# A decoder layer's ada columns, output projection and first norm: work moved between TensorE, VectorE and GpSimd

## The chip, the cores and the metric

The kernel runs on one core of a Trainium2 chip. Its time is in device microseconds (us). Five engines work beside each other, each through its own list of instructions in order, and wait for each other by semaphores: TensorE (PE, matmuls into PSUM), VectorE (DVE), ScalarE (ACT), GpSimd (Pool) and SyncE (SP), which here only starts DMAs.

## The reference

One decoder layer on x of 512 tokens x 1024, in f32:

```python
mods = silu(c) @ w_ada + b_ada                  # 6 x 1024: sh1, sc1, g1, sh2, sc2, g2
u = x * (1.0 + sc1) + sh1
z = u @ w_in                                    # q, k, v, r, low rank, 3 attention groups, 2 gates
y_gla, y_att = gla(...), dilated_attention(...)
merged = sigmoid(ga) * (y_gla @ w_proj_gla) + sigmoid(gd) * (y_att @ w_proj_attn)
x = layer_norm(alpha * x + g1 * (merged @ w_out), ln1_g, ln1_b)
u = x * (1.0 + sc2) + sh2
y = hier_moe(u, ...)                            # 1 of 4 groups, 2 of its 8 experts per token
x = layer_norm(alpha * x + g2 * y, ln2_g, ln2_b)
```

## The kernel before

**Products.** Each large f32 matmul is done as three in `float32r`: a value is split into a rounded part (`_hi`, a copy on ACT) and a remainder (`_lo`, a subtraction on DVE). Weights come from DRAM by SP in slabs of 128x1024, four to an item of 512 columns, into eight slots. ACT's `slab_hi(j)` and DVE's `slab_lo(j)` split one slab; a slot is reused when the last product that reads it is finished. Products go to PSUM banks 0 and 1 in turn, so product i waits until product i-2 is evacuated.

**Order.** `steps` is one list, written out by hand, that PE, ACT and DVE each walk in the same order, doing their own part of each step: `("z", i)` is a product and its evacuation, `("split", j)` the split of slab j. `zs_next` puts the splits of the next item between the products of this one.

**Start (until 51 us).** The scale and shift of u are the first four blocks of 512 columns of `silu(c) @ w_ada`, in the order `FIRST = (2, 3, 0, 1)`; each comes in two DMAs of 1 MB. For each block DVE multiplies the eight 128x512 slices by a number per partition and adds them (L1364, L1366), and PE sums the result over partitions with four matmuls against a column of ones (L732), so the result stands as columns. DVE adds the bias: `mcol` (L1374, L1377). In the meantime PE has transposed x, ACT copied it out (`xT`, L1022), and split slabs 0 to 3. With `mcol` ACT makes `uT_hi` (L1031), DVE the value of u in place (L1384) and its remainder `uT_lo` (L1391), both behind `uT_hi`. Then DVE splits slabs 0 to 3, and PE runs `lra` and the products of q, k, v and so on.

**Merge and output (611 to 776 us).** Eight `pg` products (y_gla by `w_proj_gla`) are multiplied by their gates on DVE. Between them lie the three parts of `combine`, in which DVE joins the attention groups (`yatt`). PE transposes `yatt` (four steps), and eight `pa` products of half the depth follow: DVE multiplies by the gate (`sgd`, L1306), adds to `mT` (L1308), ACT makes `mT_hi` and DVE `mT_lo` (L1277). The splits of the slabs of `wo` (w_out) lie among the `pa` steps. Eight `wo` products follow, two halves for each 128 tokens. At the first DVE makes the rows of the second modulation, ln1_b * (1+sc2) + sh2 and ln1_g * (1+sc2) (L1318 to L1320). After each pair of halves it has the row statistics (`row_stats`), normalises in place (L1351) and scales twice (L1354, L1355): `u2` for the experts, `x1` for the residual. Pool stores both; PE transposes `u2` and makes the router's logits, which the routing waits for.

**Experts (from 797 us).** A loop over chunks of tokens by expert, the weights split on ACT and DVE as above.

Pool (L568 to L637) starts DMAs: the rows for the modulations, the loads of `x1`, `mods`, `ln_g`, `ln_b` after the last `pg`, and `wr_sb` after the last `pa`.

Of the kernel before, what the change touches and what calls it, by code (L numbers as in the profile page):

```python
# [95 lines left out]
def build(nc, x, c_col, rel_bias, w_ada, b_ada, b_first, w_lra, w_dense, w_gla_gate, b_gla, gla_norm,  # L96
# [254 lines left out]
    between = {2: 0, 3: 1, 5: 2}  # L351
    for ct in range(KD):
        zs_next(("pg", ct, pgn[ct // 4]))
        if ct in between:
            steps.append(("combine", between[ct]))
    for t in range(4):
        z(("yattT", t, None))
    for ct in range(KD):
        if ct < 4:
            split(won[0], ct)  # L360
        elif ct % 2 == 0:
            split(won[1], ct // 2 - 2)
# [66 lines left out]
    fin_in = [sem(f"fin_in{t}") for t in range(NT)]  # L429
# [274 lines left out]
    def _(pe):  # L704
# [17 lines left out]
        for k in range(KD):  # L722
# [4 lines left out]
            last.then_inc(xT_ps, 1)  # L727
        for j in range(4):
# [498 lines left out]
    def _(dve):  # L1227
# [51 lines left out]
        def evac(i):  # L1279
# [31 lines left out]
            else:  # L1311
                t, half = q // 2, q % 2
                hs = slice(512 * half, 512 * half + 512)
                if q == 0:
                    dve.wait_ge(x1_in, 16)
                    dve.wait_ge(mods_in, 48)
                    dve.wait_ge(ln_in, 48)
                    link(dve.tensor_tensor(lnt[0][:, :], ln_b[:, :], mods[:, 2, :], ALU.mult))  # L1318
                    dve.tensor_tensor(mods[:, 1, :], lnt[0][:, :], mods[:, 1, :], ALU.add)
                    dve.tensor_tensor(mods[:, 2, :], ln_g[:, :], mods[:, 2, :], ALU.mult).then_inc(ln_used, 1)  # L1320
# [36 lines left out]
        for j in range(4):
            a = first_acc[j]
            for k in range(KD):
                if k % (KD // 2) == 0:  # L1360
# [11 lines left out]
        dve.wait_ge(small_in, 80)
        dve.wait_ge(col_ps, 2)
        link(dve.scalar_tensor_tensor(out=mcol[:, 0, :], in0=bank(6)[:, 0:KD], scalar=1.0, in1=bcol[:, 0, :],  # L1374
                                      op0=ALU.add, op1=ALU.add))
        dve.wait_ge(col_ps, 4)
        dve.tensor_tensor(mcol[:, 1, :], bank(7)[:, KD:2 * KD], bcol[:, 1, :], ALU.add).then_inc(mcol_rdy, 1)  # L1377
# [4 lines left out]
        def u_value(k):
            dve.wait_ge(u_hi, k + 1)
            dve.tensor_scalar(xT[:, k, :], xT[:, k, :], mcol[:, 0, k:k + 1], mcol[:, 1, k:k + 1], ALU.mult, ALU.add).then_inc(u_val, 1)  # L1384

        u_value(0)
        for k in range(KD):
            if k < KD - 1:
                u_value(k + 1)
            dve.wait_ge(u_val, k + 1)  # L1390
            dve.tensor_tensor(uT_lo[:, k, :], xT[:, k, :], uT_hi[:, k, :].bitcast(f32), ALU.subtract).then_inc(u_lo, 1)  # L1391
# [381 lines left out]
```

## Time and profile before

| | us |
|---|---|
| median of three runs | 1418.17 (1415.79 to 1421.04) |
| profiled execution | 1420.77 |
| its span, first to last instruction | 1418.7 |
| PE busy in the span | 1302.0 (92%) |
| DVE busy | 1023.0 (72%) |
| ACT busy | 691.9 (49%) |
| Pool busy | 364.5 (26%) |

The page of a profile gives busy times, the span in 40 slices, the chain of work that ended last, and groups of instructions. The timeline gives single instructions: start, duration, engine, line, output <- inputs, and in brackets the idle time before it and what ended it. PEld is PE's weight load, SPq the queue of SP. An f32 matmul stands as two records, one in float32r and a transpose as one.

### The profile page before, as it was taken

What the parts mean: (1) busy time and instruction counts of PE and PEld (TensorE: products, weight loads), DVE (VectorE), ACT (ScalarE), POOL (GpSimd) and SP (SyncE); (2) the same over time, 40 slices, a digit from 0 to 9 for tenths busy, and PEclk for the clock granted to TensorE, in tenths of its full rate; (3) what the DMA queues carried; (4) which work ended last, traced back from release to release, by engine and by line L of the source; (5) the groups of instructions that cost most, each with busy time, mean ns of one, the idle gap of its engine ahead of it and who ended that gap; (6) DMA issues with size and microseconds to landing.
All of it is one profiled execution on the core that took longest, in us unless ns stands there. A gap on an engine that the chain in (4) does not pass through costs nothing.

```text
span 1418.7 us, 18051 instructions
## 1 busy us (share of the span) xinstructions
PE 1302.0 (92%) x6280; PEld 1057.1 (75%) x6280; DVE 1023.0 (72%) x1103; ACT 691.9 (49%) x846; POOL 364.5 (26%) x210
## 2 busy tenths in 40 slices
PE   4899899999999999999897499999999999999990
PEld 2577676667898898888676478888888888888870
DVE  6777657744443333337697779999999999999975
ACT  2422344434333433461312267777777777777740
POOL 0100000000000000000001315655665656655532
PEclk8899999999999999999997599999999999999995
DMA  9985311103203223252516589999999999999923
GB/s 348 368 293 201 119 61 58 45 16 119 75 16 119 66 82 109 73 181 92 204 67 270 212 313 362 371 374 371 366 363 368 365 382 367 376 368 370 363 70 121
DMA packets 72866, 314.43 MB, mean 222 GB/s; under 512 B 14898, under 2 KB 15058, under 8 KB 47984
## 3 DMA queue, kind: packets, MB, share of 16 engines
q1 hardware_dynamic: 57488, 283.36, 53.6%
q0 software_dynamic: 14752, 28.29, 6.5%
q10 hardware_dynamic: 576, 2.10, 0.4%
q8 instruction: 33, 0.54, 0.1%
q14 instruction: 17, 0.14, 0.0%
HBM read 313.58 MB, written 28.95 MB: 241 GB/s over the span
## 4 chain that ended last, share of the span: by engine, by line
PE 81%; DVE 10%; ACT 3%; SPq 2%; issue 2%; DMA 2%; DVEq 0%; POOLq 0%; ACTq 0%
PE ps L945 12%; PE ps L947 12%; PE ps L946 12%; PE ps L739 11%; PE ps L741 10%; PE ps L740 10%; PE ps L866 2%; PE ps L935 2%; PE ps L908 1%; DVE d_lo L1245 1%; PE ps L844 1%; PE ps L841 1%; PE ps L962 1%; SPq L485 1%; PE ps L878 1%
## 5 line engine op out<-in xcount | busy, mean ns | idle before, releaser
L1634 DVE TENSOR_TENSOR w_lo<-w_raw,w_hi 128x2048 fp32r<-128x2048 f32 x192 | 433.1, 2286 | 24.6 <-ACT w_hi L1156 24.6
L1156 ACT CAST w_hi<-w_raw 128x2048 fp32r<-128x2048 f32 x192 | 357.3, 1917 | 0.0
L945 PE MATMUL ps<-w_hi,xT_hi 128*128 128x512 f32 x512 | 207.4, 405 | 2.4 <-DVE xT_lo L1647 2.4
L673 POOL DMA_INDIRECT y_d<-yb,ui x32 | 167.4, 5231 | 163.2 <-DVE yb L1642 138.7
L947 PE MATMUL ps<-w_hi,xT_lo 128*128 128x512 f32 x512 | 201.6, 394 | 0.0
L946 PE MATMUL ps<-w_lo,xT_hi 128*128 128x512 f32 x512 | 200.5, 392 | 0.0
L1245 DVE TENSOR_TENSOR d_lo<-d_raw,d_hi 128x1024 fp32r<-128x1024 f32 x96 | 115.1, 1222 | 75.8 <-ACT d_hi L1018 74.9
L739 PE MATMUL ps<-uT_hi,d_hi 128*128 128x512 f32 x384 | 155.7, 405 | 0.2 <-DVE d_lo L1245 0.2
L741 PE MATMUL ps<-uT_hi,d_lo 128*128 128x512 f32 x384 | 151.1, 393 | 0.0
L740 PE MATMUL ps<-uT_lo,d_hi 128*128 128x512 f32 x384 | 150.8, 393 | 0.0
L945 PEld LDWEIGHTS ps<-w_hi,xT_hi 128*128 128x128 f32 x512 | 97.1, 190 | 21.3 <-DVE xT_lo L1647 2.8
L947 PEld LDWEIGHTS ps<-w_hi,xT_lo 128*128 128x128 f32 x512 | 96.7, 189 | 21.4
L946 PEld LDWEIGHTS ps<-w_lo,xT_hi 128*128 128x128 f32 x512 | 97.4, 190 | 18.8
L945 PE MATMUL ps<-w_hi,hT_hi 128*128 128x512 f32 x256 | 100.5, 393 | 2.0 <-DVE hT_lo L1672 2.0
L739 PE MATMUL ps<-d_hi,uT_hi 128*128 128x512 f32 x224 | 93.9, 419 | 9.0 <-DVEq L1295 6.4
L1018 ACT CAST d_hi<-d_raw 128x1024 fp32r<-128x1024 f32 x96 | 97.7, 1043 | 6.4 <-DMA d_raw<-in 4.9
L946 PE MATMUL ps<-w_lo,hT_hi 128*128 128x512 f32 x256 | 100.4, 392 | 0.0
L947 PE MATMUL ps<-w_hi,hT_lo 128*128 128x512 f32 x256 | 100.4, 392 | 0.0
L605 POOL DMA_DIRECT2D bias<-brep_d x3 | 2.7, 908 | 352.0 <-DVE sm L1481 188.3
L740 PE MATMUL ps<-d_lo,uT_hi 128*128 128x512 f32 x224 | 89.4, 399 | 0.0
L739 PEld LDWEIGHTS ps<-uT_hi,d_hi 128*128 128x128 f32 x384 | 72.8, 190 | 22.1 <-issue 5.8
L741 PE MATMUL ps<-d_hi,uT_lo 128*128 128x512 f32 x224 | 89.3, 399 | 0.0
(312 smaller groups left out, 2173.5 us busy)
## 6 DMA issues: line engine op xcount, KB each, us to landing
w_raw<-in SPq DMA_DIRECT2D x192, 1024.0 KB, 7.3
d_raw<-in SPq DMA_DIRECT2D x96, 512.0 KB, 3.6
ada_buf<-in SPq DMA_DIRECT2D x8, 2048.0 KB, 8.9
ada_w<-in SPq DMA_DIRECT2D x8, 1024.0 KB, 14.1
att_d<-Og POOLq DMA_DIRECT2D x2, 1056.0 KB, 7.6
O<-att_d POOLq DMA_DIRECT2D x2, 1056.0 KB, 8.2
x_in<-in SPq DMA_DIRECT2D x1, 2048.0 KB, 13.7
brep_d<-bvec_d POOLq DMA_DIRECT2D x2, 1024.0 KB, 19.1
```

The costliest lines, as they stand in the source:

```text
L673: pool.indirect_dma_start(y_d, bass.IndirectOffsetOnAxis(ap=idxs[s], axis=0), yb[s][:, :], None, bounds_check=S - 1, oob_is_err=False, com ...
L739: pe.matmul(dst, a_hi, b_hi, start=first, stop=False)
L740: pe.matmul(dst, a_hi, b_lo, start=False, stop=False)
L741: return pe.matmul(dst, a_lo, b_hi, start=False, stop=final)
L866: last = pe.matmul(dst, lhs, rhs, start=True, stop=True)
L945: pe.matmul(dst, a_hi[:, k, :], hi[:, w], start=(k == 0), stop=False)
L946: pe.matmul(dst, a_hi[:, k, :], lo[:, w], start=False, stop=False)
L947: last = pe.matmul(dst, a_lo[:, k, :], hi[:, w], start=False, stop=(k == a_hi.shape[1] - 1))
L1018: act.copy(d_hi[j % SLOTS][:, :], d_raw[j % SLOTS][:, :]).then_inc(d_hi_rdy, 1)
L1156: act.copy(w_hi[n % NHI][:, :], w_raw[j][:, :]).then_inc(w_hi_rdy, 1)
L1245: dve.tensor_tensor(d_lo[j % SLOTS][:, :], d_raw[j % SLOTS][:, :], d_hi[j % SLOTS][:, :].bitcast(f32), ALU.subtract).then_inc(d_lo_rdy, 1)
L1634: dve.tensor_tensor(w_lo[j][:, :], w_raw[j][:, :], w_hi[n % NHI][:, :].bitcast(f32), ALU.subtract).then_inc(w_lo_rdy, 1)
```

## The change

- **Ada columns.** Of the four first blocks, DVE sums blocks 0 and 2 (`ON_DVE`) as before. Blocks 1 and 3 are multiplied and summed on PE: for each half of a block that has landed and each 128 columns, four matmuls with the weights as stationary operand and a column of silu(c) as moving one. The two halves stand in separate PSUM columns, and DVE adds them with one more operation for each of the two rows of `mcol`.
- **u.** ACT makes `uT_hi` ahead of the copies of slabs 0 to 3 instead of behind them. The values of u go to a tile of their own, `u_f32`, and no longer wait for `uT_hi`; DVE makes the first five, Pool the last three.
- **combine** stands after `pg` products 0, 2 and 4 instead of 2, 3 and 5.
- **Splits of `wo`.** Slab 0 ahead of the transposes of y_att, 1 among them, 2 behind them, 3 at the second `pa`, instead of one at each of the first four `pa`. The others stay.
- **Norm rows.** The three operations L1318 to L1320 are on Pool, behind the landing of their inputs. The load of `wr_sb` stands behind them in Pool's order.
- **Norm.** Instead of one normalising operation and two of two for scaling, `normed` does (v - mean) * g and then * rstd + b, for `u2` and for `x1`: four operations where five were.
- The semaphores of the first DMAs serve for those of the last tiles too.

```diff
-    between = {2: 0, 3: 1, 5: 2}
+    between = {0: 0, 2: 1, 4: 2}
...
+    split(won[0], 0)
     for t in range(4):
         z(("yattT", t, None))
+        if t == 1:
+            split(won[0], 1)
+    split(won[0], 2)
     for ct in range(KD):
-        if ct < 4:
-            split(won[0], ct)
-        elif ct % 2 == 0:
+        if ct == 1:
+            split(won[0], 3)
+        if ct in (4, 6):
             split(won[1], ct // 2 - 2)
...
         pool.wait_ge(mcol_rdy, 1)
+
+        pool.wait_ge(xT_sb, KD)
+        for k in range(U_POOL, KD):
+            pool.tensor_scalar(u_f32[:, k, :], xT[:, k, :], mcol[:, 0, k:k + 1], mcol[:, 1, k:k + 1], ALU.mult, ALU.add).then_inc(u_val_pool, 1)
...
+        pool.wait_ge(mods_in, 48)
+        pool.wait_ge(ln_in, 32)
+        link(pool.tensor_tensor(lnt[1][:, :], ln_b[:, :], mods[:, 2, :], ALU.mult))
+        pool.tensor_tensor(mods[:, 1, :], lnt[1][:, :], mods[:, 1, :], ALU.add)
+        link(pool.tensor_tensor(mods[:, 2, :], ln_g[:, :], mods[:, 2, :], ALU.mult))
+        pool.sem_inc(ln_used, 1)
...
         for j in range(4):
-            pe.wait_ge(first_sum, j + 1)
-            for q in range(4):
-                n = 4 * j + q
-                last = pe.matmul(bank(6 + j // 2)[:, n:n + 1], first_acc[j][:, P * q:P * q + P], ones[:, 0:1], start=True, stop=True)
+            dst = bank(6 + j // 2)
+            if j in ON_DVE:
+                pe.wait_ge(first_sum, ON_DVE.index(j) + 1)
+                for q in range(4):
+                    n = 4 * j + q
+                    last = pe.matmul(dst[:, n:n + 1], first_acc[j][:, P * q:P * q + P], ones[:, 0:1], start=True, stop=True)
+            else:
+                for h in range(2):
+                    pe.wait_ge(half_in[2 * j + h], 16)
+                    for q in range(4):
+                        n = 4 * j + q + 16 * h
+                        for k in range(KD // 2 * h, KD // 2 * h + KD // 2):
+                            last = pe.matmul(dst[:, n:n + 1], ada_w[j][:, k, P * q:P * q + P], csil[:, k:k + 1],
+                                             start=(k % (KD // 2) == 0), stop=(k % (KD // 2) == KD // 2 - 1))
             last.then_inc(col_ps, 1)
...
-        act.wait_ge(first_sum, 1)
-        for j in range(4):
-            slab_hi(j)
         act.wait_ge(mcol_rdy, 1)
         act.wait_ge(xT_sb, KD)
         for k in range(KD):
             act.activation(uT_hi[:, k, :], xT[:, k, :], ACT.Identity, bias=mcol[:, 1, k:k + 1], scale=mcol[:, 0, k:k + 1]).then_inc(u_hi, 1)
+        for j in range(4):
+            slab_hi(j)
...
-                    norm_rows(x1[:, t, :])
-                    scale_rows(u2[:, t, :], x1[:, t, :], mods[:, 2, :], mods[:, 1, :]).then_inc(u2_rdy, 1)
+                    row_stats(x1[:, t, :], lrs)
+                    normed(u2[:, t, :], x1[:, t, :], mods[:, 2, :], mods[:, 1, :]).then_inc(u2_rdy, 1)
...
+        def normed(o, v, g, b):
+
+            link(dve.scalar_tensor_tensor(out=o, in0=v, scalar=bnag[:, 0:1], in1=g, op0=ALU.subtract, op1=ALU.mult))
+            return dve.scalar_tensor_tensor(out=o, in0=o, scalar=lrs, in1=b, op0=ALU.mult, op1=ALU.add)
...
-        for j in range(4):
+        for j in ON_DVE:
...
         def u_value(k):
-            dve.wait_ge(u_hi, k + 1)
-            dve.tensor_scalar(xT[:, k, :], xT[:, k, :], mcol[:, 0, k:k + 1], mcol[:, 1, k:k + 1], ALU.mult, ALU.add).then_inc(u_val, 1)
+            dve.tensor_scalar(u_f32[:, k, :], xT[:, k, :], mcol[:, 0, k:k + 1], mcol[:, 1, k:k + 1], ALU.mult, ALU.add).then_inc(u_val, 1)
```

## Rows read from the trace of the kernel before

**Rows 1.** The page's part 4: the chain that ended last, by engine.
```profile
PE 81%; DVE 10%; ACT 3%; SPq 2%; issue 2%; DMA 2%; DVEq 0%; POOLq 0%; ACTq 0%
```

**Rows 2.** The timeline until 51 us: start, duration, engine, line, operation.
```profile
19.25 0.49 DVE L1364 TENSOR_SCALAR first_acc<-ada_w,sm 128x512 f32<-128x512 f32 x1 [4.36 <-DMA ada_w<-in]
...
31.60 5.47 DVE L1366 SCALAR_TENSOR_TENSOR first_acc<-ada_w,sm,first_acc 128x512 f32<-128x512 f32 x7
...
39.08 1.04 ACT L1018 CAST d_hi<-d_raw 128x1024 fp32r<-128x1024 f32 x1 [0.24 <-DMA d_raw<-in]
39.10 0.17 DVE L1377 TENSOR_TENSOR mcol<-ps,bcol 128x8 f32<-128x8 f32 x1 [1.96 <-PE ps L732]
...
40.03 5.75 ACT L1031 ACTIVATE uT_hi<-xT,mcol 128x512 fp32r<-128x512 f32 x8
...
50.90 0.50 PE L739 MATMUL ps<-uT_hi,d_hi 128*128 128x512 f32 x1 [0.18 <-DVE d_lo L1245]
```

**Rows 3.** The timeline of PE's matmuls, 22 to 44 us.
```profile
23.14 0.95 PE L732 MATMUL ps<-cst,first_acc 128*128 128x1 f32 x8
...
37.13 1.87 PE L732 MATMUL ps<-cst,first_acc 128*128 128x1 f32 x8 [4.04 <-DVE first_acc L1366]
```

**Rows 4.** Stretches: length, busy PE, PEld, DVE, ACT, Pool (x count), clock, DMA, GB/s.
```profile
23.00:25.00 2.00, 1.09 (x11) 1.01 (x9) 1.93 (x3) 0.76 (x2) 0.00 (x0) 1.00 1.05 386
25.00:27.00 2.00, 1.69 (x8) 1.69 (x8) 1.93 (x4) 0.00 (x0) 0.00 (x0) 0.54 1.06 388
...
45.60:46.00 0.40, 0.40 (x4) 0.09 (x1) 0.40 (x2) 0.18 (x1) 0.00 (x0) 0.95 1.03 412
...
100.00:120.00 20.00, 20.00 (x88) 16.21 (x87) 14.95 (x19) 5.56 (x7) 1.45 (x3) 1.00 0.63 218
...
766.00:770.00 4.00, 1.02 (x5) 1.02 (x6) 3.93 (x4) 0.00 (x0) 0.53 (x1) 0.50 1.01 428
...
796.00:802.00 6.00, 0.00 (x0) 0.00 (x0) 6.00 (x5) 0.00 (x0) 4.50 (x3) 0.50 0.11 29
```

**Rows 5.** The timeline of PE, 756 to 776 us.
```profile
763.65 1.98 PE L707 MATMUL ps<-wr_sb,u2T 128*128 128x36 f32 x16 [0.73 <-ACT u2T L1136]
768.98 1.97 PE L886 MATMUL ps<-cst,u 128*128 128x128 f32 x8 [3.36 <-DVE u L1355]
```

**Rows 6.** The chain of work in order of time, 600 to 800 us: start, length, what.
```profile
792.15 3.72 PE ps L926 x16
```

**Rows 7.** The timeline of DVE, 596 to 800 us.
```profile
689.08 1.22 DVE L1245 TENSOR_TENSOR d_lo<-d_raw,d_hi 128x1024 fp32r<-128x1024 f32 x1 [1.64 <-ACT d_hi L1018]
...
716.95 1.22 DVE L1318 TENSOR_TENSOR lnt<-ln_b,mods 128x1024 f32<-128x1024 f32 x1
...
720.60 0.69 DVE L1323 TENSOR_TENSOR lnt<-ps,mods 128x512 f32<-128x512 f32 x1
...
727.42 0.81 DVE L1351 TENSOR_SCALAR x<-x,sm 128x1024 f32<-128x1024 f32 x1
```

**Rows 8.** The timeline of PE, 677 to 716 us: the first matmul of the fifth `pa`.
```profile
695.32 0.50 PE L739 MATMUL ps<-yattT_hi,d_hi 128*128 128x512 f32 x1 [1.29 <-DVEq L1307]
```

**Rows 9.** The timeline of DVE, 1385 to 1420 us.
```profile
1405.00 1.28 DVE L1712 SCALAR_TENSOR_TENSOR ya<-ya,sm,ln2gb 128x1024 f32<-128x1024 f32 x1
1406.20 3.36 DVE L1710 SCALAR_TENSOR_TENSOR ya<-ya,sm,ln2gb 128x1024 f32<-128x1024 f32 x1
```

**Rows 10.** The timeline of Pool, 1370 to 1420 us.
```profile
1405.20 3.28 POOL L700 TENSOR_TENSOR ya<-ya,ln2gb 128x1024 f32<-128x1024 f32 x1 [18.00 <-ACT ya L1220]
1408.56 3.20 POOL L701 TENSOR_TENSOR ya<-ya,ln2gb 128x1024 f32<-128x1024 f32 x1
```

**Rows 11.** The timeline of Pool, 596 to 800 us.
```profile
775.32 1.96 POOL L640 MEMSET xg<- 128x1024 f32 x2 [3.17 <-PE ps L707]
```

**Rows 12.** The instructions that touch `ln_b`: its load and that DMA's time to landing.
```profile
L627 POOL DMA_DIRECT2D ln_b<-in x1: 528/528/528, 681.6 to 681.6; - x1
...
DMA to landing us min/median/max: 15.5/15.5/15.5
```

More of the change, by code:

```diff
@@ L128, in build @@
     x_in = at("x_in", 112, [P, NT, D])
+    u_f32 = at("u_f32", 112, [P, KD, S])
+    U_POOL = 5
     ada_w = [at(f"ada_w{b}", kb, [P, KD, 512]) for b, kb in enumerate((64, 80, 160, 176))]
@@ L399, in build @@
     csil_act = sem("csil_act")
-    first_in = [sem(f"first_ada_in{n}") for n in range(8)]
+    half_in = [sem(f"first_ada_half_or_last_tile_in{n}") for n in range(8)]
     xT_ps, xT_sb, col_ps, mcol_rdy = sem("xT_ps"), sem("xT_sb"), sem("mod_cols_ps"), sem("mod_cols")
     first_sum = sem("first_ada_sum")
-    FIRST = (2, 3, 0, 1)
+    FIRST, ON_DVE = (2, 3, 0, 1), (0, 2)
+    csil_rdy = sem("csil_rdy")
     out_rdy, out_act, out_dve, sig_rdy = sem("out_rdy"), sem("out_freed_act"), sem("out_freed_dve"), sem("sig_rdy")
@@ L428, in build @@
     y_st = [sem("y_store0"), sem("y_store1")]
-    fin_in = [sem(f"fin_in{t}") for t in range(NT)]
     fin_rdy, ln2_in, last_rdy = sem("fin_rdy"), sem("ln2_in"), sem("last_rdy")
@@ L484, in _ @@
                 ks = slice(KD // 2 * h, KD // 2 * h + KD // 2)
-                sp.dma_start(ada_w[j][:, ks, :], cols(w_ada, 512 * b)[:, ks, :]).then_inc(first_in[2 * j + h], 16)
+                sp.dma_start(ada_w[j][:, ks, :], cols(w_ada, 512 * b)[:, ks, :]).then_inc(half_in[2 * j + h], 16)
             if j == 0:
@@ L1241, in _ @@
         link(dve.tensor_tensor(csil, csil, ccol, ALU.mult))
+        dve.sem_inc(csil_rdy, 1)
         def slab_lo(j):
@@ L1315, in evac @@
                     dve.wait_ge(x1_in, 16)
[L1316 to L1320, printed above, removed]
                     dve.wait_ge(ln_used, 1)
@@ L1371, in _ @@
                     ins.then_inc(first_sum, 1)
[L1372 to L1377, printed above, removed]
         dve.wait_ge(lra_hi_rdy, 1)
         dve.tensor_tensor(lra_lo[:, :, :], lra_w[:, :, :], lra_hi[:, :, :].bitcast(f32), ALU.subtract).then_inc(lra_lo_rdy, 1)
+        dve.wait_ge(small_in, 80)
+        for m, add in ((0, 1.0), (1, 0.0)):
+            dve.wait_ge(col_ps, 2 * m + 2)
+            c = bank(6 + m)
+            link(dve.scalar_tensor_tensor(out=mcol[:, m, :], in0=c[:, KD * m:KD * m + KD], scalar=add, in1=bcol[:, m, :],
+                                          op0=ALU.add, op1=ALU.add))
+            ins = dve.tensor_tensor(mcol[:, m, KD // 2:KD], mcol[:, m, KD // 2:KD],
+                                    c[:, 16 + KD * m + KD // 2:16 + KD * m + KD], ALU.add)
+            if m == 0:
+                link(ins)
+            else:
+                ins.then_inc(mcol_rdy, 1)
         dve.wait_ge(mcol_rdy, 1)
+        dve.wait_ge(xT_sb, KD)
         def u_value(k):
-            dve.wait_ge(u_hi, k + 1)
-            dve.tensor_scalar(xT[:, k, :], xT[:, k, :], mcol[:, 0, k:k + 1], mcol[:, 1, k:k + 1], ALU.mult, ALU.add).then_inc(u_val, 1)
+            dve.tensor_scalar(u_f32[:, k, :], xT[:, k, :], mcol[:, 0, k:k + 1], mcol[:, 1, k:k + 1], ALU.mult, ALU.add).then_inc(u_val, 1)
         u_value(0)
         for k in range(KD):
-            if k < KD - 1:
+            if k < U_POOL - 1:
                 u_value(k + 1)
-            dve.wait_ge(u_val, k + 1)
-            dve.tensor_tensor(uT_lo[:, k, :], xT[:, k, :], uT_hi[:, k, :].bitcast(f32), ALU.subtract).then_inc(u_lo, 1)
+            if k < U_POOL:
+                dve.wait_ge(u_val, k + 1)
+            else:
+                dve.wait_ge(u_val_pool, k - U_POOL + 1)
+            dve.wait_ge(u_hi, k + 1)
+            dve.tensor_tensor(uT_lo[:, k, :], u_f32[:, k, :], uT_hi[:, k, :].bitcast(f32), ALU.subtract).then_inc(u_lo, 1)
         for j in range(4):
```

18 lines of the change are left out of this document (7 added, 11 removed).

## The prediction

> **What bounds the kernel now.** I read the page's chain first [rows 1]: TensorE (PE) holds 81% of it and VectorE (DVE) 10%. So a microsecond saved on another engine counts only where PE waits for that engine, and a microsecond added ahead of PE's first dense work counts in full if PE is dense afterwards. It is: in the stretch from 100 to 120 us PE is busy for 20.00 of 20.00 us [rows 4]. The change touches two places where PE does wait, so I then read the timeline of the first 51 us and that of the output projection (677 to 776 us).
>
> In the first place the ada columns come out of four weight blocks. DVE multiplies and adds eight slices for each block, 0.49 us and then 7 in 5.47 us; the fourth block's seven start at 31.60 and `mcol` is finished at 39.10 + 0.17 = 39.27 [rows 2]. At 40.03 ACT starts the eight `uT_hi`, after its last slab copy (39.08 + 1.04) [rows 2], and the first product of q starts at 50.90 [rows 2]: T + 11.6, with T = 39.27 for `mcol`. In the second place DVE and ACT hold PE up: PE stood for 1.29 us ahead of the fifth product of `pa` [rows 8], because of the slab splits between the gates.
>
> **Edit 1: blocks 1 and 3 summed on PE. The price of one call.** A call is an f32 matmul with a 128x128 stationary block of `ada_w` and one moving column of `csil`. The trace has this very shape, L732: four calls are 8 records, and take 0.95 us at 23.14 and 1.87 us at 37.13 [rows 3]. The clock tells them apart: granted 1.00 from 23 to 25 us and falling to 0.50 after (mean 0.54 from 25 to 27) [rows 4], that is 2.4 against 1.2 GHz. So a call costs 0.24 us at 2.4 GHz and 0.47 us at 1.2 GHz, although one column moves: the stationary side is what is paid. Block 1 now needs 2 halves x 4 quarters x 4 slices = 32 calls where it had 4, and block 3 the same: 7.7 or 14.9 us for each block.
>
> Which clock? PE will be busy without a break, but with one-column work. I read what such work did to the clock. Before 25 us it did transposes and eight records of one column, then little, and the clock fell. After a run of sixteen 128x36 matmuls that ended at 763.65 + 1.98 = 765.63 the clock was 0.50 in the next stretch [rows 5, 4]. Sixteen short matmuls without a pause, 3.72 us at 792.15 [rows 6], didn't lift it: 0.50 from 796 to 802 [rows 4]. The 128x512 matmuls of `lra` did: 0.95 in the stretch from 45.6 us on [rows 4]. I therefore take 1.2 GHz from 25.2 us on. This is the choice on which the forecast hangs.
>
> Order on PE: the transposes end at 23.14, block 0 takes 0.95 (24.1); block 1 runs 1.1 us at the high clock (9 of its 64 records) and 55 records x 1.87/8 = 12.9 us at the low one: 38.1. Block 2's sum must be there: its halves land at 24.7 and 27.4, since the first half of block 1 was there at 19.25 [rows 2] and at 386 GB/s [rows 4] a 1.05 MB half takes 2.7 us; DVE ends it near 30.7, unwaited for. Block 2 takes 1.9 (40.0), block 3 64 x 0.234 = 15.0 (its last half landed near 32.8, so it isn't late): 55.0. Two short column operations on DVE instead of one, 0.17 us each as at 39.10 [rows 2], give T = 55.3. **Against 39.27 that is +16.0 us.** DVE has 2 x 5.96 us less to do, but stands idle for it: its sums are not what is late. Bounds: if the clock falls some us later, each us at the high clock saves one; I allow 3, so +13 to +17. If it never falls: 24.1 + 7.7 + 1.0 + 7.7 + 0.3 = 40.8, +1.5.
>
> The Trainium skill speaks against my choice: "TensorE: Matmul & The Clock Gate", section "Why this matters for your kernels", has it that keeping TensorE continuously busy brings the full clock. The row at 792.15 disagrees, with 3.72 us of work and 0.50 behind it; by the rule the sum would be the rival below.
>
> **Edit 2: u by three engines, slab copies behind it.** ACT starts `uT_hi` at T + 0.05 instead of T + 0.76 and takes 0.72 a piece; its first slab copy ends at T + 6.9, in time. DVE does five values (0.46 each, back to back) and eight remainders (0.60) instead of eight and eight, but no longer waits for `uT_hi` at the start. Pool makes three values 128x512. The trace shows none; the nearest rows are its memset of 128x1024, 1.96 us for two [rows 11], so 0.5 us for half of one, and its two-input 128x1024, 2.2 us alone (below), so 1.1 for half. I take the middle, 0.8. Pool's operation and DVE's with two SBUF inputs don't run side by side (next edit), so I add them: the first remainder at T + 1.0, four values and seven remainders more, Pool's three 0.8 each in between: last remainder at T + 9.7, first `d_lo` at T + 10.8. Against T + 11.6 **-0.8 us** (0 to -1.7 for 1.1 and 0.5). DMAs that wait for `mcol` (`gn_b`, `mrow`, the `brep` copies behind Pool's three operations) are needed 100 us later.
>
> "GPSIMD Engine Reference" of the Trainium skill, section 3.1, gives 0.77 us for 512 elements in its best loop; by it the sum would be the same.
>
> **Edit 3: norm rows folded on Pool.** DVE loses three operations at 716.95 until 720.60 [rows 7], 3.65 us. What Pool's cost is shows at the end of the trace. Pool's 128x1024 product was issued at 1405.20 while DVE's operation of 1405.00 ran (1.28 us, until 1406.28), and ended at 1408.48: 2.2 us alone [rows 9, 10]. DVE's next, of 1406.20, took 3.36 us instead of 1.28, so it waited until Pool had finished; Pool's second, of 1408.56, then ended 2.2 us after DVE's end at 1409.56 [rows 9, 10]. So whoever has begun keeps the other out. The inputs land at 681.6 + 15.5 = 697.1 [rows 12]: Pool runs three times 2.2 us from 697 on, in the midst of `pa`, where DVE's `mT`, `mT_lo` and `d_lo` have two SBUF inputs. I followed DVE, ACT and PE in order through this stretch with durations of [rows 7, 8]; the same recurrence, run for the order of before, ends the last remainder of m at 714.3 and the last logits at 775.2, as the trace has them.
>
> **Edit 4: slab splits and combines earlier.** Three of the six splits of `wo` within `pa` go. A step with a split is a chain of 4.3 us: twice 0.69 and 0.15 for the gate (a 128x512 operation takes 0.69 at 720.60), 0.5 for ACT's `mT_hi`, half of a slab copy, 1.04 for that copy and 1.14 to 1.22 for `d_lo`, as at 689.08 [rows 7]. One without is three operations of 0.69 on DVE, 2.05. Two cycles saved give -4.5; the two splits now among the transposes of y_att cost +0.6: -3.9 for the last `mT_lo`, 710.4. The combines stay beside PE's dense `pg` products, whose banks DVE can empty one product late: nothing, and if one came too late, the wait of DVE behind it would be PE's.
>
> With Pool in it: its 6.6 us cost DVE 4.9 (the rest falls beside `sgd`, which reads PSUM, and waits for ACT). The last `mT_lo` is at 715.3, the second product of `wo` ends at 722.0 and DVE's second evacuation at 723.7, where it was: the 3.65 us removed only replace a wait for PE.
>
> **Edit 5: norm in two operations.** For each row tile the 0.81 us operation at 727.42 [rows 7] and four of 1.23 become four of 1.28. Ahead of the fourth u2 that is -0.7 us, and another 0.5 comes from bank waits that PE has less of. The last transposes start at 768.98 [rows 5]; now at 767.5. **Edits 3 to 5: -1.2 us**, to -6.1 if Pool does not hold DVE up, to 0 if it does so more.
>
> **Sum:** +16.0 - 0.8 - 1.2 = +14.0 us. The profiled execution took 1420.77 (span 1418.7, and 2.1 around it): 1434.8. It lies 2.6 above the median of the runs, 1418.17, so for a median I say **1432**. Own range: +13 - 1.7 - 6.1 to +17, 1423 to 1435.
>
> **Rivals.** (a) The clock stays at 2.4 GHz through the one-column work. For it: PE has no pause. Against it: the three rows above. Then +1.5 - 0.8 - 1.2 = -0.5, 1418, between 1412 and 1421: not slower. It decides as soon as PE's records of block 1 keep 0.12 us each beyond 26 us. (b) A call that adds to the same column costs less than one that stands alone. No row has this. At its limit the last half's landing decides, T = 32.8 + 0.9: -5.6 - 0.8 - 1.2 = -7.6, 1410.6, faster. Against it: 128x36 matmuls, which do add up eight deep, cost 1.98/16 = 0.12 us a record [rows 5], no less than L732. (c) The clock falls, but returns or stays for part of the 64 + 64 records: half of the price, +6, about 1424. (d) Edits 3 to 5 give their whole 6.1 us because Pool gets its turns where DVE idles; with the forecast's start that is 1427, in its own range.
>
> **Chances.** The forecast with (d) 0.76, (a) 0.10, (b) 0.05, (c) 0.09. Low end 1420, to hold (c) and part of (a), high end 1436. This kernel's measurement can tell about 0.5% from nothing, 7.1 us: slower than 1425.3 is the forecast less its lowest end, 0.74, and a third of (c), 0.03; faster than 1411.1 is (b), 0.05; the rest is 0.18.
>
> **What would show it.** Right: PE's records of the ada columns at 0.23 us with a granted clock of 0.50, `mcol` near 55 us, the first q product near 66; DVE idle from 31 us. Pool's three products of 2.2 to 3.3 us around 697 to 706 with DVE operations of 2 to 3 us beside them; wo's second evacuation still near its old place, apart from the shift of the start. Wrong: records of 0.12 us with clock 1.00, or far fewer us for 64 records, or DVE operations of 0.7 us beside Pool's.

## The result, and the profile after

The changed kernel takes 1429.53 us (median of 6 runs, 1428.89 to 1430.12), the kernel before 1419.16 us beside it (6 runs, 1415.79 to 1421.04): a ratio of 1.0071, 95% interval 1.006 to 1.0081. It is slower by 10.4 us. The profiled execution of after took 1428.89 (span 1426.7), that of before 1420.77 (span 1418.7): 8.1 apart, less than the medians, because before's was one of its slower runs and after's its fastest.

By engine, the chain of after against [rows 1]: PE's share has grown by four points, DVE's and ACT's have shrunk.

```profile
PE 85%; DVE 9%; ACT 2%; DMA 2%; issue 1%; SPq 0%; DVEq 0%; POOLq 0%; ACTq 0%
```

The two places of the change, first the ada columns. The timeline of PE's matmuls of after, 19 to 51 us (start, duration, line, count), answers to [rows 3]:

```profile
18.70 3.95 PE L743 MATMUL ps<-cst,x_in 128*128 128x128 f32 x22
22.49 0.95 PE L752 MATMUL ps<-cst,first_acc 128*128 128x1 f32 x8
23.30 10.92 PE L759 MATMUL ps<-sm,ada_w 128*128 128x1 f32 x64
34.08 1.85 PE L752 MATMUL ps<-cst,first_acc 128*128 128x1 f32 x8
35.78 13.79 PE L759 MATMUL ps<-sm,ada_w 128*128 128x1 f32 x64
```

L759 is the new work, block 1 and block 3. The stretches of after over the same time (length, busy PE, PEld, DVE, ACT, Pool with counts, granted clock, DMA, GB/s) answer to [rows 4]:

```profile
22.40:25.00 2.60, 2.60 (x27) 2.60 (x25) 0.44 (x1) 0.81 (x2) 0.00 (x0) 1.00 1.05 388
25.00:28.00 3.00, 3.00 (x23) 3.00 (x22) 2.86 (x5) 0.00 (x0) 0.00 (x0) 0.75 1.05 386
28.00:31.00 3.00, 3.00 (x16) 3.00 (x15) 2.45 (x4) 0.00 (x0) 0.00 (x0) 0.50 1.05 386
...
36.00:40.00 4.00, 4.00 (x20) 4.00 (x21) 0.00 (x0) 0.00 (x0) 0.00 (x0) 0.50 1.03 418
45.00:49.00 4.00, 4.00 (x20) 4.00 (x21) 0.00 (x0) 0.00 (x0) 0.00 (x0) 0.50 0.98 360
```

PE is busy for every microsecond of it, and the granted clock falls all the same, from 2.4 to 1.2 GHz between 25 and 28 us, and stays there. The records come at 27 in 2.60 us before the fall and at 16 in 3.00 us behind it. DVE and Pool wait for it. Their timelines of after, 49 to 62 us, against [rows 2]:

```profile
49.68 0.17 DVE L1398 SCALAR_TENSOR_TENSOR mcol<-ps,bcol 128x8 f32<-128x8 f32 x1 [14.77 <-PE ps L759]
49.88 0.16 DVE L1400 TENSOR_TENSOR mcol<-mcol,ps 128x4 f32<-128x4 f32 x1
...
50.99 1.10 DVE L1421 TENSOR_TENSOR uT_lo<-u_f,uT_hi 128x512 fp32r<-128x512 f32 x1
52.02 0.54 DVE L1410 TENSOR_SCALAR u_f<-xT,mcol 128x512 f32<-128x512 f32 x1
52.47 1.09 DVE L1421 TENSOR_TENSOR uT_lo<-u_f,uT_hi 128x512 fp32r<-128x512 f32 x1
...
55.42 3.08 DVE L1421 TENSOR_TENSOR uT_lo<-u_f,uT_hi 128x512 fp32r<-128x512 f32 x5
```
```profile
50.23 4.27 POOL L585 TENSOR_SCALAR u_f<-xT,mcol 128x512 f32<-128x512 f32 x3 [36.46 <-DVE mcol L1400]
```

DVE stood idle for 14.77 us and `mcol` was ready at 49.88 + 0.16 = 50.04 instead of 39.27. The first product of q started at 60.20 instead of 50.90: 9.3 us of the loss are there by 61 us.

The second place. Pool's three new operations, then what DVE (696 to 736 us) and PE (710 to 716 us) did meanwhile, in the timelines of after, against [rows 7, 8]:

```profile
704.39 2.58 POOL L641 TENSOR_TENSOR lnt<-ln_b,mods 128x1024 f32<-128x1024 f32 x1 [13.99 <-DMA ln_b<-in]
707.05 2.73 POOL L642 TENSOR_TENSOR mods<-lnt,mods 128x1024 f32<-128x1024 f32 x1
709.74 2.79 POOL L643 TENSOR_TENSOR mods<-ln_g,mods 128x1024 f32<-128x1024 f32 x1
```
```profile
704.02 0.68 DVE L1305 TENSOR_TENSOR mT_lo<-mT,mT_hi 128x512 fp32r<-128x512 f32 x1
704.62 0.68 DVE L1334 TENSOR_TENSOR sgd<-ps,sgd 128x512 f32<-128x512 f32 x1
705.45 2.06 DVE L1336 TENSOR_TENSOR mT<-mT,sgd 128x512 f32<-128x512 f32 x1
707.44 2.89 DVE L1305 TENSOR_TENSOR mT_lo<-mT,mT_hi 128x512 fp32r<-128x512 f32 x1
710.25 3.35 DVE L1273 TENSOR_TENSOR d_lo<-d_raw,d_hi 128x1024 fp32r<-128x1024 f32 x1
...
727.99 0.69 DVE L1346 TENSOR_TENSOR lnt<-ps,mods 128x512 f32<-128x512 f32 x1
728.72 0.69 DVE L1347 SCALAR_TENSOR_TENSOR x<-x,lnt 128x512 f32<-128x512 f32 x1
733.33 0.69 DVE L1346 TENSOR_TENSOR lnt<-ps,mods 128x512 f32<-128x512 f32 x1 [3.92 <-PE ps L769]
```
```profile
714.32 0.80 PE L767 MATMUL ps<-yattT_hi,d_hi 128*128 128x512 f32 x1 [4.49 <-DVEq L1335]
```

The same `mT_lo` takes 0.68 us when it starts ahead of Pool's first operation and 2.89 beside the second, and PE then waits 4.49 us. DVE has lost the 3.65 us of the row operations of [rows 7], and waits 3.92 us for PE at the second evacuation of `wo`. From the first `pg` evacuation to the first exponential of the routing the trace has 137.39 us before (639.68 to 777.07) and 138.93 after (647.96 to 786.89).

### The profile page after: what moved, and what is told of

It is laid out like the page before. It is cut to its first block, busy times and chain, and to the rows that moved or that the text cites. A ratio compares the mean times of both kernels' runs of the same rounds, so it can differ in the third digit from the quotient of the medians.

```text
span 1426.7 us, 18264 instructions
## 1 busy us (share of the span) xinstructions
PE 1321.9 (93%) x6392; PEld 1079.1 (76%) x6392; DVE 1011.2 (71%) x1079; ACT 692.2 (49%) x846; POOL 370.7 (26%) x216
## 4 chain that ended last, share of the span: by engine, by line
PE 85%; DVE 9%; ACT 2%; DMA 2%; issue 1%; SPq 0%; DVEq 0%; POOLq 0%; ACTq 0%
PE ps L973 12%; PE ps L975 12%; PE ps L974 12%; PE ps L767 12%; PE ps L769 11%; PE ps L768 11%; PE ps L894 2%; PE ps L963 2%; PE ps L759 2%; PE ps L936 1%; PE ps L872 1%; PE ps L869 1%; PE ps L990 1%; DVE d_lo L1273 1%; DMA x_in<-in 1%
## 5 line engine op out<-in xcount | busy, mean ns | idle before, releaser
L690 POOL DMA_INDIRECT y_d<-yb,ui x32 | 161.0, 5033 | 159.4 <-DVE yb L1672 134.9
L1046 ACT CAST d_hi<-d_raw 128x1024 fp32r<-128x1024 f32 x96 | 97.7, 1043 | 16.8 <-DMA d_raw<-in 15.2
## 6 DMA issues: line engine op xcount, KB each, us to landing
x_in<-in SPq DMA_DIRECT2D x1, 2048.0 KB, 13.7
```

The source lines that it names most:

```text
L690: pool.indirect_dma_start(y_d, bass.IndirectOffsetOnAxis(ap=idxs[s], axis=0), yb[s][:, :], None, bounds_check=S - 1, oob_is_err=False, com ...
L1046: act.copy(d_hi[j % SLOTS][:, :], d_raw[j % SLOTS][:, :]).then_inc(d_hi_rdy, 1)
```

## The experiments

Two theories stood. A: the ada sums on PE are the whole loss, 10.7 us as seen at `mcol`, and everything else is a small gain. C: Pool's fold of the norm rows holds DVE up and eats what edits 3 to 5 would give. The rivals were that the late edits or a shifted clock cause the loss, and that Pool's part is harmless.

**Ada sums back on DVE, all else as changed.** The second column operation stays, as an addition of zero. The cuts of the code here and below show the lines that matter; "..." stands where some are left out.

```diff
-    FIRST, ON_DVE = (2, 3, 0, 1), (0, 2)
+    FIRST, ON_DVE = (2, 3, 0, 1), (0, 1, 2, 3)
...
```

> The changed kernel with all four ada blocks summed on VectorE again (the PE sums undone), all else of the change kept. Theory A (the price of the 64 one-column calls on PE is the whole loss): mcol is ready at 39.3 us instead of 50.04, and everything behind it moves by 10.7 us: 1429.5 - 10.7 = 1418.8, equal to the kernel before within 2 us. Rival B (the loss lies mostly in the late edits): 1424 or more.

Measured: 1415.86 us (10 runs), ratio 0.9985 (0.997 to 1.0001), 13.7 below the changed kernel by the medians. `mcol` was ready at 39.68, the first q product started at 50.36, 9.8 earlier than in after. Theory A holds: the loss is gone. The median is 2.9 below the 1418.8 that theory A gave; the part on the prediction says what that difference is made of. Pool and DVE still held each other up, since Pool still folds the rows; the timeline of this kernel, 692 to 700 us:

```profile
694.86 0.69 DVE L1305 TENSOR_TENSOR mT_lo<-mT,mT_hi 128x512 fp32r<-128x512 f32 x1
...
695.91 2.40 POOL L641 TENSOR_TENSOR lnt<-ln_b,mods 128x1024 f32<-128x1024 f32 x1 [14.66 <-DMA ln_b<-in]
...
696.29 2.57 DVE L1336 TENSOR_TENSOR mT<-mT,sgd 128x512 f32<-128x512 f32 x1
```

**Edit 1 alone.** The kernel before, with blocks 1 and 3 summed on PE and nothing else.

> The kernel before with nothing but blocks 1 and 3 summed on PE. Theory A: mcol ready near 50 us, first q product at 50.0 + 11.6 = 61.6 or somewhat sooner, because the slab copies are done by then (uT_hi starts 0.7 earlier after mcol): 60.9; time 1419.2 + 10.0 to 10.7 = 1429.5. Rival B: below 1425.

Measured: 1430.23 us (4 runs), ratio 1.0071 (1.0043 to 1.0099), 11.2 above the kernel before. `mcol` was ready at 52.40 (+13.1) and the first q product started at 63.28 (+12.4), both more than 2 us later than expected. Its block 1 took more than after's, 13.01 us, because the clock fell sooner: the mean granted clock was 0.72 from 24 to 25 us and 0.50 from 25 us on. In the timeline of PE's matmuls, 20 to 66 us:

```profile
23.56 13.01 PE L742 MATMUL ps<-sm,ada_w 128*128 128x1 f32 x64
36.43 1.84 PE L735 MATMUL ps<-cst,first_acc 128*128 128x1 f32 x8
38.14 13.79 PE L742 MATMUL ps<-sm,ada_w 128*128 128x1 f32 x64
```

Edit 1 by itself makes the loss. Block 3 costs 13.79 us in both kernels; when the clock falls differs from one trace to the next, and nothing here shows why.

**Can filling work hold the clock?** After every four calls, one 128x512 matmul into a bank that nobody reads, and one of 16 columns behind each block; that work is extra. It reads a piece of `uT_hi` that ACT copies out of x first, and PE waits for that copy ahead of block 0.

```diff
+        pe.wait_ge(warm_rdy, 1)
...
+                        pe.matmul(bank(0), uT_hi[:, 0, 0:P], uT_hi[:, 0, :], start=True, stop=True)
...
```

> The changed kernel with one extra 128x512 float32r matmul into an unused bank after every four of the one-column calls (8 more for each block), whose result nobody reads. Theory A1 (the calls of block 1 and 3 are slow because the granted clock falls to 1.2 GHz during one-column work): the clock stays at 1.00, a call costs 0.24 us, a block 7.7 + 8 x 0.23 = 9.5 us, mcol is ready at 23.4 + 9.5 + 1.0 + 9.5 + 0.4 = 43.8 us instead of 50.0, time 1429.5 - 6.2 = 1423.3. Rival A2 (the calls cost what they cost, whatever the clock): 16 x 0.4 us more work, mcol at 56, time 1436.

Measured: 1441.73 us (4 runs), ratio 1.0164 (1.0142 to 1.0186), beyond both theories' numbers. The clock was not held. The stretches of this kernel:

```profile
25.00:28.00 3.00, 3.00 (x17) 2.90 (x16) 2.86 (x5) 0.00 (x0) 0.00 (x0) 0.54 1.05 386
28.00:31.00 3.00, 3.00 (x16) 2.90 (x14) 2.59 (x4) 0.00 (x0) 0.00 (x0) 0.50 1.05 386
```

PE had paused 1.24 us just before, for the copy that the edit itself brought in (22.4 to 25 us: 1.17 busy of 2.60), so this doesn't tell whether the filling would hold a clock that is up; it didn't lift one that was down, in 36 us. A group of eight records with its filling came every 2.13 us (29.47, 31.60, 33.73), about 0.4 more than eight records back to back in after (8 x 0.215).

**One block on PE instead of two.** Block 1 on PE, block 3 back on DVE.

```diff
-    FIRST, ON_DVE = (2, 3, 0, 1), (0, 2)
+    FIRST, ON_DVE = (2, 3, 0, 1), (0, 2, 3)
...
```

> The changed kernel with only block 1 on PE, blocks 0, 2 and 3 on VectorE. VectorE's third sum ends at 24.6 + 2 x 5.96 = 36.5, PE has been done with block 1 since 34.2, then four calls for block 2 and four for block 3, 1.9 us each at 1.2 GHz: mcol at 38.4 + 0.4 = 38.8. Theory A: 1429.5 - 11.2 = 1418.3. Rival: the sum of three blocks on VectorE is late by itself and mcol is no sooner than 42: 1421 or more.

Measured: 1417.68 us (10 runs), ratio 0.9992 (0.9978 to 1.0006); `mcol` at 40.56 (38.8 was expected), 0.9 behind the kernel with all four on DVE. The first q product started at 50.21, no later than the 50.36 of that kernel. Its timelines, 20 to 50 us, PE and DVE:

```profile
23.91 12.76 PE L759 MATMUL ps<-sm,ada_w 128*128 128x1 f32 x64
36.53 3.55 PE L752 MATMUL ps<-cst,first_acc 128*128 128x1 f32 x16
```
```profile
31.10 2.33 DVE L1386 SCALAR_TENSOR_TENSOR first_acc<-ada_w,sm,first_acc 128x512 f32<-128x512 f32 x3
34.26 3.11 DVE L1386 SCALAR_TENSOR_TENSOR first_acc<-ada_w,sm,first_acc 128x512 f32<-128x512 f32 x4 [0.84 <-DMA ada_w<-in]
```

The first block's 12.8 us on PE lie beside DVE's sums, which end at 37.37, and cost nothing that the time shows; only the second block, whose weights land last, has nothing beside it. That is where the price is paid.

**The other operand order.** The same sums with `silu(c)` as the one-column stationary operand and the 128x512 slices of `ada_w` moving: 8 calls for a block, a copy of the row by ACT, and 4 calls that turn it back into columns.

```diff
...
-                            last = pe.matmul(dst[:, n:n + 1], ada_w[j][:, k, P * q:P * q + P], csil[:, k:k + 1], ...
...
+                    last = pe.matmul(bank(j // 2)[0:1, :], csil[:, k:k + 1], ada_w[j][:, k, :], ...
...
```

> The changed kernel with the operands of the ada calls swapped: the column of silu(c) is stationary, 128x512 slices of the block move (8 calls of 512 columns for a block instead of 32 of one), ACT copies the row out of PSUM, four calls of one row turn it into columns. Theory A (the price is the stationary loads, doubled because one-column work lets the clock fall): the clock stays at 1.00 through block 1; a record of 512 f32 columns takes 0.43 us at 2.4 GHz (33x384 took 0.64 at 1.2), 16 records 6.8 us; mcol near 23.4 + 6.8 + 0.7 + 0.5 + 0.95 + 6.8 + 0.7 + 0.5 + 0.4 = 40.8 us, time 1429.5 - 9.2 = 1420.3. Rival (PE is throttled by something else, the DMA load or f32 itself): the clock is 0.50, 13.6 us a block, mcol at 54, time 1433.

Measured: 1421.27 us (10 runs), ratio 1.0022 (1.0007 to 1.0037), 8.3 below the changed kernel. Its timeline of PE's matmuls and two of its stretches:

```profile
23.99 7.03 PE L757 MATMUL ps<-ada_w,sm 128*1 128x512 f32 x16
31.69 1.05 PE L762 MATMUL ps<-cst,first_acc 1*128 1x1 f32 x8 [0.67 <-ACT first_acc L1054]
32.66 1.05 PE L752 MATMUL ps<-cst,first_acc 128*128 128x1 f32 x8
33.65 7.03 PE L757 MATMUL ps<-ada_w,sm 128*1 128x512 f32 x16
```
```profile
25.00:28.00 3.00, 3.00 (x9) 0.59 (x7) 2.86 (x5) 0.00 (x0) 0.00 (x0) 1.00 1.05 387
37.00:40.00 3.00, 3.00 (x8) 0.59 (x7) 0.00 (x0) 0.00 (x0) 0.00 (x0) 1.00 1.01 403
```

With 512 columns moving PE kept 2.4 GHz through both blocks, beside the same DMA traffic, and a block took 7.03 us instead of 13.79. So it isn't that traffic, nor f32 as such, that takes the clock down in the changed kernel. `mcol` was ready at 42.66 (40.8 was expected), still 3.0 later than with DVE's sums.

**Norm rows back on DVE (and ada sums on DVE).** Pool's three operations go back to DVE, ahead of the first evacuation of `wo`; the router weights' load gets its own semaphore.

```diff
-        link(pool.tensor_tensor(lnt[1][:, :], ln_b[:, :], mods[:, 2, :], ALU.mult))
-        pool.tensor_tensor(mods[:, 1, :], lnt[1][:, :], mods[:, 1, :], ALU.add)
-        link(pool.tensor_tensor(mods[:, 2, :], ln_g[:, :], mods[:, 2, :], ALU.mult))
...
+                    link(dve.tensor_tensor(lnt[1][:, :], ln_b[:, :], mods[:, 2, :], ALU.mult))
+                    dve.tensor_tensor(mods[:, 1, :], lnt[1][:, :], mods[:, 1, :], ALU.add)
+                    dve.tensor_tensor(mods[:, 2, :], ln_g[:, :], mods[:, 2, :], ALU.mult).then_inc(ln_used, 1)
```

> All ada blocks on VectorE (as in e1_ada_dve, 1415.9) and the three norm-row operations back on VectorE too, at their old place ahead of the first output evacuation; all else of the change kept. Theory C (Pool's three products of 2.2 us lock VectorE out in the midst of pa, and PE stands behind that): the mT additions of 2 to 2.6 us and the PE pauses of 4.5 us among pa vanish, the last mT_lo comes 4.9 us sooner, the rows cost 3.65 of it on VectorE but beside PE's second output product; the second evacuation 3.5 to 4 sooner: 1412. Rival D (Pool's help is worth its place, what it blocks was idle): 1416 to 1419.

Measured: 1412.09 us (10 runs), ratio 0.9953 (0.9936 to 0.997), 3.8 below the same kernel with the rows on Pool by the medians (5.0 by the means, with a 95% interval of 2.6 to 7.4), and below the kernel before. From the first `pg` evacuation to the routing it takes 134.62 us instead of 139.21. In its timeline of DVE, 695 to 730 us, no operation is stretched:

```profile
699.44 0.69 DVE L1299 TENSOR_TENSOR mT_lo<-mT,mT_hi 128x512 fp32r<-128x512 f32 x1
...
709.81 1.22 DVE L1340 TENSOR_TENSOR lnt<-ln_b,mods 128x1024 f32<-128x1024 f32 x1
711.06 1.23 DVE L1341 TENSOR_TENSOR mods<-lnt,mods 128x1024 f32<-128x1024 f32 x1
712.20 1.22 DVE L1342 TENSOR_TENSOR mods<-ln_g,mods 128x1024 f32<-128x1024 f32 x1
713.45 0.69 DVE L1345 TENSOR_TENSOR lnt<-ps,mods 128x512 f32<-128x512 f32 x1
```

Theory C holds: with the move to Pool the kernel is longer, although it took 3.65 us off DVE.

**The rows on DVE, one step later,** between the first and the second evacuation of `wo`, so that the first bank comes free sooner.

> As e5_rows_dve, but the three operations stand between the first and the second output evacuation, where VectorE stood idle for 3.9 us in the changed kernel. Theory C: as e5 or up to 1 us better, 1411 to 1412. Rival D: no better than 1416.

Measured: 1413.06 us (10 runs), ratio 0.9952 (0.9935 to 0.9969): not to be told from the kernel just above. Its first-`pg`-to-routing stretch was 133.65 us, 1.0 less, a size that the medians don't show.

**All u values on DVE (ada sums on DVE, rows on Pool).**

```diff
-    U_POOL = 5
+    U_POOL = 8
```

> As e1_ada_dve with all eight values of u on VectorE, none on Pool. Theory: Pool's three values took 4.27 us there and stretched VectorE's remainders from 0.68 to 1.09 us, so that the first q product came 10.7 us after mcol; without Pool eight values at 0.46 and eight remainders at 0.60 make 8.5 us and the first slab 1.2: first q product 10.0 to 10.3 after mcol, 1415.5, the same as e1 within what can be measured. Rival (Pool's part is worth its 3 x 0.46 us): 1417.3.

Measured: 1418.19 us (10 runs), ratio 1.0 (0.9987 to 1.0014). Against the 1415.86 of the kernel with three values on Pool this leans the other way, but both kernels' runs spread over 5 to 6 us. In the traces `mcol` was ready at 39.66 and q's first product started 9.8 us later. In the traces of after and of seven kernels with Pool's three values (all but the one with filling work) it is 9.65 to 10.7 us, longest where `lra` ran longest at 0.50, so neither a gain nor a loss from Pool's part is shown.

**The old order of slab splits** (ada sums and rows on DVE): six splits of `wo` within `pa`, none among the transposes of y_att, and the combines at their old places.

> The kernel with the ada sums and the norm rows on DVE (1412.09 us), with the old order of slab splits and combines: six splits of wo within pa, none among the transposes of y_att. Splits theory (step 4 of the prediction): two slab cycles come back into pa and the splits leave the transposes, -4.5 + 0.6 taken back, so +3.9: 1416.0 us, and first output row to routing (134.6 us from the first pg evacuation in that kernel) gets 138.5. Clock theory (the splits among the transposes lengthen PE's thin stretch, and the clock falls for the first pa products, which costs 2 us of the gain): without them the clock holds, the first pa gate is done 3.9 us after the last yattT_lo instead of 6.9, and the net is +1.9: 1414.0 us, 136.5 us. If the order is worth nothing: 1412.

Measured: 1416.41 us (12 runs), ratio 0.998 (0.9968 to 0.9992), 4.3 above the same kernel with the new order (4.3 by the means too, interval 2.1 to 6.5). The splits theory said 1416.0. From the first `pg` evacuation to the routing the trace has 137.59 us (it said 138.5) against 134.62. The clock theory falls: the fall came here too, with nothing between the transposes. The stretches of this kernel, then those of before:

```profile
680.00:682.00 2.00, 0.66 (x4) 0.42 (x4) 1.29 (x2) 1.58 (x3) 1.51 (x3) 1.00 0.88 217
682.00:684.00 2.00, 1.76 (x6) 1.47 (x7) 1.31 (x2) 0.24 (x1) 0.00 (x0) 0.77 1.00 410
684.00:686.00 2.00, 2.00 (x6) 1.52 (x6) 0.00 (x0) 0.00 (x0) 0.00 (x0) 0.50 1.01 416
```
```profile
682.00:684.00 2.00, 1.13 (x5) 0.98 (x6) 1.79 (x2) 0.87 (x1) 0.13 (x1) 1.00 0.99 403
684.00:686.00 2.00, 2.00 (x11) 1.63 (x10) 0.22 (x2) 0.00 (x0) 0.00 (x0) 1.00 1.02 422
```

**Both middle splits behind the four transposes** (ada sums and rows on DVE).

> The kernel with the ada sums and the norm rows on DVE (1412.09 us), with the splits of wo's slabs 1 and 2 both after the four transposes of y_att instead of one between them and one behind. Clock theory: PE's pause of 1.1 us between second and third transposes goes and the clock holds at 1.00 for the first pa products; the first pa gate is done 3.9 instead of 6.9 us after the last yattT_lo: 1.1 + 2 to 3 us less, 1409 to 1410 us. Theory that the fall is chance or comes from elsewhere (the pause before the first pa product, which waits for yattT_lo and stays): only the 1.1 us, if DVE's second d_lo doesn't hold the first gate up: 1411 us, with 0.50 to 0.63 in the first 2 to 4 us of pa.

Measured: 1412.04 us (6 runs), ratio 0.9942 (0.9927 to 0.9957), the same as with the splits among the transposes (1412.09). PE's pause of 1.08 us between the second and third transposes stayed, so no split between them made it; DVE was still at the split of slab 0, which stands ahead of them (1.22 us from 675.40), and the first remainder of y_att came behind it, at 676.53. The splits' clock theory is out, since the clock fell again (0.82 from 678 to 680 us, 0.50 from 680 to 686). The 1411 us of the other theory can't be told from 1412.04.

## Why the prediction was right, and where its terms were off

It said 1432 and slower; it was 1429.53. The cause that it named for the loss is shown twice, by a kernel without edit 1 and by one with nothing else. Pool's hold on DVE and the worth of the new order are shown by kernels without them. Edits 2 and 5 have no kernel of their own; they are read from traces.

That the number came so near is in part luck. In the profiled executions the change cost 8.1 us where the sum had 14.0: it was 5.9 too high by the first q product (+9.3 against +15.2), 2.7 too low from the first `pg` evacuation to the routing (+1.5 against -1.2), and after is 1.0 shorter than before between these two places and 1.8 shorter behind the routing, where the change alters no work. The last two are not explained.

**Edit 1, +16.0 forecast; +10.8 by `mcol` against before, and +9.8 by the first q product against the kernel without it, in the profiled executions; +13.7 by the medians of with and without.** The choice on which the forecast hung, 1.2 GHz for one-column work, was right: 64 records took 13.79 us at 0.50. The rows that it was drawn from were weaker than that: PE had idle time in the stretches in which the clock fell (1.02 us busy of 4.00 from 766 to 770), and the 3.72 us at 792.15 came after a long wait; none shows a clock that falls under work without a pause, as after's does. Rival (a), a clock that stays, fell; rival (b), cheaper calls that add up, fell too. Rival (c), half of the price, fell: the high clock lasted 1.3 us longer and never came back. Three sizes were off. (1) The transposes and block 0 ended at 23.3 instead of 24.1. (2) The clock fell about 26.5, not at 25.2: from 25 to 28 us there are 23 records, at a mean clock of 0.75. That is chance as far as the traces show, since in the kernels with edit 1 alone and with one block block 1 took 13.0 and 12.8 us, not 10.92. (3) A record back to back at 1.2 GHz costs 13.79 / 64 = 0.215 us. I took 1.87 / 8 = 0.234, but 1.87 is the time of a lone group of eight, with its start and end; over 64 records that is 1.2 us, and about 1.0 over block 1. Block 1 so ended at 34.2 instead of 38.1, and block 3 took 1.2 less: 5.1 of the 5.3 us between the forecast 55.3 and 50.04.

The medians say 13.7 for edit 1 where the traces say 9.8. Behind the first q product the profiled executions of the two kernels take the same time, 1366.5 us in after (1426.7 - 60.20) and 1367.0 in the kernel without edit 1 (1417.4 - 50.36). After's six runs lie within 1.3 us of each other. The ten runs without edit 1 fall apart: six took 1414.28 to 1416.65 with a mean granted clock of 0.957 to 0.960, and four, the profiled one (1419.59) among them, 1419.03 to 1420.42 with 0.953 to 0.955. Against those four, whose median is 1419.48, after is 10.0 longer. So some 10 us are the ada sums, up to 12.4 where the clock falls as early as in the kernel with edit 1 alone, and the rest is that six of ten runs had a higher clock somewhere else. Why none of after's six did isn't shown.

The Trainium skill's rule in "TensorE: Matmul & The Clock Gate", section "Why this matters for your kernels", that TensorE kept busy comes to full speed, isn't borne out for this work: PE was busy for 4.00 of 4.00 us at 0.50 from 36 to 40 and from 45 to 49 us. The same section's advice for thin matmuls, to pad them, was not tried: the filling work is other matmuls between them, and brought no rise of the clock.

**Edit 2, T + 10.8 forecast, T + 10.2 measured.** The mechanism held: DVE's first three `uT_lo` took 1.10, 1.09, 1.09 instead of 0.69 beside Pool's values, 1.2 us together. The terms that the prediction names add up to T + 9.4 for the last remainder, not to its 9.7. Pool's three values took 4.27 us, 1.42 each, where I had 0.8 and at most 1.1; but DVE's pairs of value and remainder came just as far apart (52.02, 53.49, 54.96), so the 1.42 may hold waits for DVE, and no trace has such a value of Pool's with DVE idle. Its own price stays open; what it cost DVE, 0.4 us a value, was half of the 0.8. Of the 1.4 us against before's T + 11.6, 0.7 come with the late `mcol` alone, since ACT's slab copies are done by then: the kernel with edit 1 and nothing else has T + 10.9.

**Edit 3.** Forecast: Pool's three at 2.2 to 3.3 us each with DVE operations of 2 to 3 us beside them, 4.9 us lost on DVE. Measured: 2.58, 2.73, 2.79, and 2.06, 2.89, 3.35 beside them instead of 0.69, 0.68, 1.22. That is 5.7 us, less what would have been waiting: relative to the first `pg` evacuation the last `mT_lo` ended 4.1 us later in after (725.36 - 647.96 = 77.4) than with the rows on DVE (707.27 - 633.96 = 73.3). The prediction's 723.7 for the second evacuation of `wo`, "where it was", is the end of its two operations. It started so in before, in the timeline of DVE, 596 to 800 us:

```profile
722.16 0.69 DVE L1323 TENSOR_TENSOR lnt<-ps,mods 128x512 f32<-128x512 f32 x1
```

In after it started at 733.33, or 725.05 less the shift of 8.28: 2.9 us later and not where it was. With the rows on DVE it started 4.3 us sooner than in after, counted from the first `pg` evacuation (715.02 - 633.96 = 81.1 against 85.4). By medians the rows on Pool cost 3.8 us; I had said 4.9 for the lock (-1.2 against -6.1), or 3.5 to 4 once DVE does the rows. PE's stall of 4.49 us also took the clock down (0.66 from 710 to 720 us), which I hadn't counted.

The Trainium skill, page "SBUF — State Buffer", section "SBUF: two separate sides", says that Pool and a DVE operation with two SBUF inputs exclude each other for a whole instruction; the rows of Pool and DVE from 704 to 713 us agree, `sgd`, which reads PSUM, keeping its 0.68.

**Edit 4, -3.9 forecast; -4.3 by the medians** of the kernels with new and old order. In the traces the splits among the transposes cost 0.5 us (forecast 0.6), the last `yattT_lo` ending 43.5 and 43.0 us after the first `pg` evacuation. From there to the end of the last `mT_lo` it is 33.26 us with the old order (682.09 to 715.35) and 28.75 with the new one in the kernel with the rows one step later (681.69 to 710.44), whose clock fell for about as long: 4.5, as forecast. The 4.3 us of a step with a split is the distance in the trace; the terms listed for it add up to 4.8, because half of the slab copy is in them twice.

**Edit 5, -1.2 forecast; -1.34 measured:** from the first evacuation of `wo` to the routing it is 56.47 us before (720.60 to 777.07) and 55.13 with the rows on DVE (713.45 to 768.58), and 55.11 with the old order too (721.54 to 776.65).

**What the sum missed** in the profiled execution is the clock's fall behind the transposes of y_att. Before's profiled execution didn't have it, after's and those of the ten kernels above did, with the old order too, and with edit 1 alone, where nothing near it is changed; so the new order doesn't make it. In the traces edits 3 to 5 read as +1.5 (138.93 against 137.39) where the medians have -3.2 for all edits but the first (1419.03 to 1415.86; forecast -2.0), with an interval of that ratio, 0.997 to 1.0001, that just holds no gain at all. I sought its cause in the splits, and that was wrong; why before's was spared, in the one trace there is of it, stays open.

The medians' -3.2 for edits 2 to 5 and +13.7 for edit 1 give the measured +10.4 by construction, since they share the kernel between them. A check of its own is the kernel with edit 1 alone: +11.2 and -3.2 make +8.0, 2.4 below the measured, within the spread of its four runs. Without Pool's fold, edits 2, 4 and 5 gave -7.05 (1419.14 to 1412.09); the prediction's steps make -0.8 - 3.9 - 1.2 = -5.9.

## What to carry to other kernels

A matrix-vector product on the PE with the weights stationary pays for 128x128 loads to move one column, and it can run at the low clock although PE never pauses, as 13.79 us at 0.50 did here; price it from back-to-back records at the low clock, and if PE must do it, let the weights be the moving operand. Work moved off an engine that isn't late (DVE's sums) onto the one that is on the path to the end costs its full length, unless, as with the first block here, the old engine still has work beside it. Before moving an operation from VectorE to GpSimd look at what VectorE runs at that moment: with two SBUF inputs on both sides they took turns, and three operations of 1.22 us came back as 3.8 us lost.

## What the runs showed of the hardware that was not expected

- f32 matmuls with a 128x128 stationary and one moving column: two records a call, 0.215 us each back to back at 1.2 GHz, about 0.10 at 2.4 GHz (27 in 2.60 us). With the roles swapped, one column stationary and 128x512 f32 moving, 0.44 us a record at 2.4 GHz (16 in 7.03 us), and the clock stayed at 1.00.
- A 128x512 matmul after every eight short records (some 0.4 us more for each group) did not raise the clock from 0.50 in 36 us, while the 128x512 matmuls of `lra` back to back raised it in every trace, their records going from 0.63 to 0.39 us.
- Pool's 128x512 multiply-add with two scalars for each partition took 1.42 us beside DVE, whose own pairs came every 1.47 us; its 128x1024 product took 2.40 to 2.79 us beside DVE.
- The granted clock fell behind the y_att transposes, where PE pauses, in all traces but one. The first `pa` matmuls then came 0.43 instead of 0.23 us apart: 1.5 us lost by this count in after, nearly 3 with the rows on DVE. Before and the kernel with edit 1 alone have the same instructions there, and only the second fell.
